# Attention's gates behind all pairs, and two of the convolution's four channel tiles on GpSimd

## What is computed

```python
for l in range(2):
    p = rms_norm(x, norm_w[l]) @ w_in[l]
    qa, ka, va, za, ub, zb, qkv_c, b_c, a_c, zc = split(p)
    oa = sliding_window_sink_attention(rope(norm(qa)), rope(norm(ka)), va, sinks[l]) * silu(za)   # 12 heads of 64
    a, gt = split(ub)                                # 512 channels each
    h = a * sigmoid(gt)
    h = causal_depthwise_conv(h, b_conv_w[l]) + b    # 31 taps over time, per channel
    ob = (silu(layer_norm(h)) @ pw_w[l] + pw_b[l]) * silu(zb)
    oc = rms_norm(gated_deltanet(qkv_c, b_c, a_c)) * silu(zc)   # has its own convolution of 4 taps
    x = x + concat(oa, ob, oc) @ w_out[l]
```

## Time and profile before

| | us |
|---|---|
| time, median of 3 runs (3611.47 to 3616.95) | 3613.13 |
| the profiled execution's own time | 3615.81 |
| its span, first to last instruction | 3614.0 |
| PE busy | 3472.0 |
| DVE busy | 2281.3 |
| ACT busy | 1851.8 |
| POOL busy | 155.6 |

### The profile page before, as it was taken

How to read it: one execution, slowest core, us unless ns; L and a number is a source line. 1 busy time by engine, 2 the same in 40 slices (tenths; PEclk the granted TensorE clock), 3 DMA queues, 4 the chain that set the end, 5 groups by cost and what they waited for, 6 DMA issues and landing times.

```text
span 3614.0 us, 41537 instructions
## 1 busy us (share of the span) xinstructions
PE 3472.0 (96%) x16074; PEld 2790.4 (77%) x16074; DVE 2281.3 (63%) x3126; ACT 1851.8 (51%) x2526; POOL 155.6 (4%) x243
## 2 busy tenths in 40 slices
PE   7988999988999999999999999999999999999998
PEld 5767778767778777788888888887777888888886
DVE  4956565966565656566666666656655566666665
ACT  4564555564555355655454454453566555445444
POOL 3014000013000000000000000000000000000000
PEclk9999999999999999999999999999999999999999
DMA  7434436434446345455655655653444565565564
GB/s 206 138 105 126 128 130 192 141 104 121 130 138 196 105 127 141 138 187 180 192 180 186 193 180 186 192 174 100 145 134 152 191 192 181 186 192 181 186 192 151
DMA packets 399092, 578.51 MB, mean 160 GB/s; under 512 B 25473, under 2 KB 222585, under 8 KB 398256
## 3 DMA queue, kind: packets, MB, share of 16 engines
q1 hardware_dynamic: 392544, 557.93, 50.4%
q0 software_dynamic: 5904, 16.75, 1.6%
q10 hardware_dynamic: 448, 1.18, 0.1%
HBM read 570.78 MB, written 4.98 MB: 159 GB/s over the span
## 4 chain that ended last, share of the span: by engine, by line
PE 82%; DVE 11%; ACT 4%; issue 2%; DMA 1%; DVEq 0%; ACTq 0%; SPq 0%
PE PS L706 79%; PE PS L703 3%; DVE WL L1844 3%; DVE ZA L2035 2%; ACT WH L1310 1%; DVE AR L1984 1%; DVE AR L2304 0%; ACT L1573 0%; DMA RAW<-in_w_in 0%; DVE SM L2243 0%; DMA X<-in_x 0%; DVE AR L2241 0%; ACT AR L1573 0%; ACT AR L1336 0%; ACT AR L1655 0%
## 5 line engine op out<-in xcount | busy, mean ns | idle before, releaser
L1844 DVE TENSOR_TENSOR WL<-RAW,WH 128x1024 fp32r<-128x1024 f32 x1056 | 1291.8, 1228 | 976.2 <-ACT WH L1310 973.6
L1310 ACT ACTIVATE WH<-RAW 128x1024 fp32r<-128x1024 f32 x1056 | 1105.1, 1056 | 965.6 <-PE PS L706 585.7
L706 PE MATMUL PS<-WH,Ah 128*128 128x512 f32 x3520 | 1431.9, 407 | 46.4 <-DVE WL L1844 32.9
L706 PE MATMUL PS<-WL,Ah 128*128 128x512 f32 x3520 | 1387.5, 394 | 0.0
L706 PE MATMUL PS<-WH,Al 128*128 128x512 f32 x3520 | 1387.4, 394 | 0.0
L706 PEld LDWEIGHTS PS<-WH,Ah 128*128 128x128 f32 x3520 | 671.9, 191 | 217.5 <-issue 40.8
L706 PEld LDWEIGHTS PS<-WL,Ah 128*128 128x128 f32 x3520 | 670.4, 190 | 145.4
L706 PEld LDWEIGHTS PS<-WH,Al 128*128 128x128 f32 x3520 | 672.3, 191 | 138.8 <-issue 6.8
L706 PE MATMUL PS<-WH,Zh 128*128 128x512 f32 x704 | 281.2, 399 | 0.0
L706 PE MATMUL PS<-WL,Zh 128*128 128x512 f32 x704 | 279.0, 396 | 0.0
L706 PE MATMUL PS<-WH,Zl 128*128 128x512 f32 x704 | 278.8, 396 | 0.0
(11 more groups left out here) (319 smaller groups left out, 2157.2 us busy)
## 6 DMA issues: line engine op xcount, KB each, us to landing
RAW<-in_w_in SPq DMA_DIRECT2D x368, 512.0 KB, 3.7
RAW<-in_w_up SPq DMA_DIRECT2D x704, 256.0 KB, 3.1
RAW<-in_w_down SPq DMA_DIRECT2D x176, 512.0 KB, 4.1
RAW<-in_w_out SPq DMA_DIRECT2D x64, 512.0 KB, 3.6
RAW<-in_w_o SPq DMA_DIRECT2D x64, 512.0 KB, 3.7
RAW<-in_w_in SPq DMA_DIRECT2D x64, 256.0 KB, 3.1
AR<-in_c POOLq DMA_DIRECT2D x2, 1600.0 KB, 7.6
AR<-bias_scratch POOLq DMA_DIRECT2D x16, 192.0 KB, 4.6
```

The lines of the kernel that those rows point to most:

```text
L706: return T.matmul(o, lhs, rhs, start=start, stop=stop, skip_group_check=True)
L1310: act(WH[:, j % NW, 0:n], raw_view(j), ACT.Copy).then_inc(*w_hi())
L1844: tt(WL[:, j % NW, 0:w], raw_view(j), WH[:, j % NW, 0:w].bitcast(F32), SUB).then_inc(*w_lo())
```

## The change

`C1CH` has zb ahead of za0. Attention's pipeline waits for va alone; DVE puts each pair's result times 0.5 into a new tile OA, and when the last pair is done and both gates are there, two products over all pairs put it into GT (gate0 over the two channel tiles of va's gate, gate1 over the four of za0); `merged` waits for gate1. In the convolution DVE keeps channel tiles 0 and 1. GpSimd does tiles 2 and 3 ahead of `base`: for each tap one product of HB with the tap into BTAP and one sum into ACC, each over both tiles, each waiting for the one before. PE's mean waits for both engines. ACT's part of DeltaNet behind the norms comes one pump later (12 + 9 instead of 12 + 8).

```diff
--- before.py
+++ after.py
@@ -209,7 +209,7 @@
 C1CH = [("uba", [(2048, 512)]), ("ubg", [(2560, 512)]), ("ba", [(5888, 12)]), ("qkv0", [(3584, 512)]), ("qkv1", [(4096, 512)]),
         ("qkv2", [(4608, 512)]), ("qa0", [(0, 512)]), ("qa1", [(512, 512)]), ("qkv3", [(5120, 512)]),
         ("qkv4", [(5632, 256), (5900, 256)]), ("zc", [(6156, 512)]), ("va", [(1024, 256), (1792, 256)]),
-        ("za0", [(1280, 512)]), ("zb", [(3072, 512)])]
+        ("zb", [(3072, 512)]), ("za0", [(1280, 512)])]
 C2CH = [("gqk", [(3072, 512)]), ("gv", [(3584, 512)]), ("ga", [(4608, 32)]), ("gr", [(4096, 512)]),
         ("dq0", [(0, 512)]), ("dk0", [(1024, 512)]), ("dv0", [(2048, 512)]), ("dq1", [(512, 512)]),
         ("dk1", [(1536, 512)]), ("dv1", [(2560, 512)]), ("rqk", [(4640, 512)]), ("rv", [(5152, 512)]),
@@ -421,7 +421,9 @@
         b_act = steps("b_act", per_layer(["id0", "id1", "id2", "id3", "sq", "vln", "vrs", "af0", "af1", "af2", "af3", "th",
                                           "pb0", "pb1", "pb2", "pb3"]))
         b_pe = steps("b_pe", per_layer(["mean", "var", "pw0", "pw1"]))
-        b_dve = steps("b_dve", per_layer([f"t{j}_{c}" for j in range(30) for c in R4] + ["mu", "cen", "nrm", "si", "out"]))
+        b_dve = steps("b_dve", per_layer([f"t{j}_{c}" for j in range(30) for c in R2] + ["mu", "cen", "nrm", "si", "out"]))
+
+        b_pool = steps("b_pool", per_layer([f"{n}{j}" for j in range(30) for n in "mt"]))
 
         items = [(t, h0) for t in (1, 0) for h0 in range(0, 12, 2)]
         aa_, ap, ad = ["sq", "ln", "rs"], [f"qt{c}" for c in range(5)], ["ss", "qn"]
@@ -441,6 +443,7 @@
             if 0 <= i - 3 < 12:
                 ap += [f"pv{i - 3}"]
                 ad += [f"gt{i - 3}"]
+        ad += ["gate0", "gate1"]
         a_act, a_pe, a_dve = steps("a_act", per_layer(aa_)), steps("a_pe", per_layer(ap)), steps("a_dve", per_layer(ad))
 
         fa, fp, fd = [], [], []
@@ -580,6 +583,8 @@
         KS, PW = za(1024, 2, 256), ar(14336, 4, 512)
         RT = [za(1024 + 128 * i, 128).rearrange("p (h d) -> p h d", d=8) for i in R4]
         SBUFS = [ar(12288 + 512 * i, 512) for i in R4]
+        OA = ar(0, 6, 256)
+        BTAP = ar(16384, 2, 256)
         OB = [ar(9216, 512), ar(0, 512)]
         OSQ = [ar(9728, 512), ar(512, 512)]
         TMP, TMF, ACC, HB, TB = za(0, 2, 512), za(0, 1024), za(1024, 4, 256), za(2048, 4, 256), za(2048, 4, 256)
@@ -857,7 +862,8 @@
                 yield from e.until("set up", "ubg")
                 for _ in range(31):
                     yield
-                T.wait_ge(*b_dve.at(m("t29_3")))
+                T.wait_ge(*b_dve.at(m("t29_1")))
+                T.wait_ge(*b_pool.at(m("t29")))
                 for c in R4:
                     ins = mm(bank(7, 256), ONES[:, :], ACC[:, c, :], c == 0, c == 3)
                 ins.then_inc(*b_pe(m("mean")))
@@ -1057,7 +1063,7 @@
                 T.wait_ge(*c_act.at(m("hl2")))
                 for i in range(15):
                     if i == 3:
-                        yield from e.until("va", "va.z", "za0")
+                        yield from e.until("va")
                     if i < 12:
                         t, h0 = items[i]
                         W = 128 + 128 * t
@@ -1097,6 +1103,8 @@
                                          SBUFS[(i - 3) % 4][:, o:o + 128], k == 0, k == t)
                         ins.then_inc(*a_pe(m(f"pv{i - 3}")))
                     yield
+                yield from e.until("va.z", "za0")
+                yield
                 e.flags.add("a")
 
             def gla(l):
@@ -1481,7 +1489,7 @@
                     if first:
                         A.wait_ge(*w_used.at(chunks[last_h[r]].end))
                         first = False
-                    A.wait_ge(*{"c": lambda: c_dve.at(f"{l}.hg12"), "b": lambda: b_dve.at(f"{l}.out"), "a": lambda: a_dve.at(f"{l}.gt11"),
+                    A.wait_ge(*{"c": lambda: c_dve.at(f"{l}.hg12"), "b": lambda: b_dve.at(f"{l}.out"), "a": lambda: a_dve.at(f"{l}.gate1"),
                                 "gla": lambda: g_dve.at(f"{l}.gg11"), "diff0": lambda: d_dve.at(f"{l}.og11"),
                                 "diff1": lambda: d_dve.at(f"{l}.og31"), "ret": lambda: r_dve.at(f"{l}.og11")}[name]())
                     for k in tiles:
@@ -1574,7 +1582,7 @@
                     A.wait_ge(*c_act.at(m(f"nln{r}")))
                     act(NS[r % 3], NS[r % 3], ACT.Exp, scale=-0.5).then_inc(*c_act(m(f"nrs{r}")))
                     yield
-                for _ in range(12 + 8):
+                for _ in range(12 + 9):
                     yield
                 for g in R3:
                     A.wait_ge(*c_pe.at(m(f"ta{g}")))
@@ -2027,7 +2037,7 @@
                 yield
                 for j in range(30):
                     d = 30 - j
-                    for c in R4:
+                    for c in R2:
                         if j == 0:
                             V.wait_ge(*b_act.at(m(f"id{c}")))
                         else:
@@ -2228,9 +2238,7 @@
                 yield from e.until("c")
                 for i in range(15):
                     if i == 3:
-                        yield from e.until("va", "va.z", "za0")
-                    if i == 3:
-                        V.wait_ge(*e_dve.at(m("za0.g")))
+                        yield from e.until("va")
                     if i < 12:
                         t, h0 = items[i]
                         W, b = 128 + 128 * t, i % 4
@@ -2256,10 +2264,16 @@
                         tt(s3, s3, ARS[b].unsqueeze(2).broadcast_to([128, 2, W]), MUL).then_inc(*a_dve(m(f"nm{i - 1}")))
                     if 0 <= i - 3 < 12:
                         t, h0 = items[i - 3]
-                        gt = GT[:, h0 // 2, 128 * t:128 * t + 128]
                         V.wait_ge(*a_pe.at(m(f"pv{i - 3}")))
-                        stt(gt, bank(4 + (i - 3) % 4, 128), 0.5, gt, MUL, MUL).then_inc(*a_dve(m(f"gt{i - 3}")))
-                    yield
+                        ts(OA[:, h0 // 2, 128 * t:128 * t + 128], bank(4 + (i - 3) % 4, 128), 0.5, None, MUL).then_inc(*a_dve(m(f"gt{i - 3}")))
+                    yield
+                yield from e.until("va.z", "za0")
+                V.wait_ge(*a_dve.at(m("gt11")))
+                for i, (j, name) in enumerate(((4, "va"), (0, "za0"))):
+                    V.wait_ge(*e_dve.at(m(name + ".g")))
+                    gt = GT[:, j:j + 4 - 2 * (j // 4), :]
+                    tt(gt, gt, OA[:, j:j + 4 - 2 * (j // 4), :], MUL).then_inc(*a_dve(m(f"gate{i}")))
+                yield
                 e.flags.add("a")
 
             def gla(l):
@@ -2565,6 +2579,15 @@
                     for h in range(8):
                         G.wait_ge(*u_dve.at(f"row{h}"))
                         G.dma_start(scr[h], BIASROW[h]).then_inc(scr_in, 16)
+                G.wait_ge(*b_act.at(f"{l}.id3"))
+                for j in range(30):
+                    n = 226 + j
+                    taps = P(("bcw", l), 4 * j + 2, 2).unsqueeze(2).broadcast_to([128, 2, n])
+                    if j > 0:
+                        G.wait_ge(*b_pool.at(f"{l}.t{j - 1}"))
+                    G.tensor_tensor(BTAP[:, :, 0:n], HB[:, 2:4, 0:n], taps, MUL).then_inc(*b_pool(f"{l}.m{j}"))
+                    G.wait_ge(*b_pool.at(f"{l}.m{j}"))
+                    G.tensor_tensor(ACC[:, 2:4, 256 - n:256], BTAP[:, :, 0:n], ACC[:, 2:4, 256 - n:256], ADD).then_inc(*b_pool(f"{l}.t{j}"))
                 base(l)
             for l in LL:
                 G.wait_ge(*p_lo.at(8 * (2 + 2 * l)))
```

## The result

The changed kernel took 3646.4 us, median of 4 runs (3645.59 to 3647.82), beside 3614.45 of the kernel before on the same chip (3611.47 to 3616.95). The ratio is 1.0098, with a 95% interval of 1.0086 to 1.0110: slower by some 32 us by the medians, or 35 by the ratio, where 47 were forecast. The profiled execution took 3646.66 with a span of 3644.8, 30.8 longer than before's.

A forecast was written before the change was run, and what follows sets the result against it. TensorE, busy 96% of the span, was taken to bound the kernel. Per layer, 27.5 (convolution) - 3 (attention) - 1 (ACT's place) = 23.5 us, 47 in all on the median 3613.1: 3660, range 3600 to 3700.

The forecast's parts named there:

- The mechanism: Convolution: DVE operations with two SBUF inputs take turns with GpSimd's; those with one PSUM input go untouched; +27.5 us a layer.
- The rival without turns: Convolution: scalar_tensor_tensor, or this shape, shares with GpSimd without loss; -18.3 us a layer, 3577; chance 0.18.
- GpSimd's operation, 1.13 us: Convolution on GpSimd: each product or sum takes 1.13 us at the mean of 482 elements, bounds 1.0 and 1.6.
- GpSimd becomes the wait: Mean after the convolution: at 2.2 us an operation it waits for GpSimd; +70 us a layer, 3750; chance 0.06.
- Price of a turn, 0.93: Convolution: a DVE operation loses all but 0.2 us of a GpSimd operation, 0.93 us for one of 1.13.
- Number of turns up to the first evacuation, 32: Pumps 0 to 8: 24 turns plus 4 at short operations plus 4 in the evacuation pump, costing 29.8 us.
- From there to GpSimd's end, +9.0: Six pumps after the first evacuation, 4.7 us each: 12.2 us later, less 3.2 of DVE's lead; PE 32.0 late.
- Second evacuation, -1.7: Convolution, GpSimd silent: the evacuation meets a lead of one pump only and costs 1.7 us less.
- Relief, 14.3: Convolution: halving DVE's steps gives PE back at most 14.3 us a layer, at the first three stalls and the mean.
- ACT one place later, -1: DeltaNet behind the norms: ACT issues its next weight tile before waiting for the transposes; -1 us a layer (0 to -2).
- Attention, -3: Attention's new order: 6.7 us saved at the change to the projection, some given back; net -3 a layer (0 to -7).
- The clock: Long convolution pumps: PE idle 2 of 4.7 us might lower its clock to 0.50; up to +7 us a layer, 3675.

The follow-up runs named there:

- experiment 5: Kernel before with all its DVE convolution steps, plus GpSimd's 60 operations a layer on a copy nobody uses, which PE's mean waits for: 3684.97 us, ratio 1.0199.
- experiment 8: Kernel before with only attention's new order (zb ahead of za0, gates behind all pairs), ACT at 12 + 8: 3609.43 us, ratio 0.9991.
- experiment 1: Kernel before with only the convolution of two channel tiles moved to GpSimd; attention and ACT's place as before: 3657.38 us, ratio 1.0135.
- experiment 3: Kernel before with only ACT's part of DeltaNet one pump later (12 + 9): 3602.17 us, ratio 0.9979.
- experiment 4: Changed kernel without GpSimd's convolution loop, leaving out all but the last tap of channel tiles 2 and 3: 3581.41 us, ratio 0.9927.
- experiment 6: Changed kernel with 120 GpSimd fills a layer in place of its products and sums, so it writes but reads nothing: 3578.98 us, ratio 0.9909.
- experiment 2: Changed kernel with all four channel tiles on DVE, keeping attention's new order and ACT's 12 + 9: 3601.21 us, ratio 0.9977.
- experiment 7: Changed kernel with one channel tile on GpSimd and three on DVE, 60 operations a layer of half the elements: 3611.53 us, ratio 0.9999.

## Why the prediction was right in kind and too high

PE's lateness in layer 0, tile by tile against the earlier trace rows, shows where the terms held. It sets one execution beside one, and the execution before is off in two places. From 94 to 97.5 us, ahead of GpSimd's first operation, it has a granted clock of 1.00, the changed kernel 0.57 and experiments 5 and 8 0.56 and 0.55; so its tile at 105.94 starts 1.0 to 1.5 us earlier than in the changed kernel and in experiments 1, 3, 5 and 8. From 265.75 to 388.90 it takes 4.0 to 4.2 us more than experiments 1, 5 and 8, whose kernels are those of the one before in this stretch. So some 1.3 us of the rows up to the mean is not the change's, and the last row is some 3 too low.

| place (start before, start after) | forecast | measured |
|---|---|---|
| tile after first evacuation (138.17, 156.04) | +23.0 | +17.9 |
| GpSimd's last operations (159.84, 184.82) | +32.0 | +25.0 |
| after the second evacuation (174.70, 199.89) | +30.3 | +25.2 |
| norm sums, third evacuation (191.42, 214.59) | +28.3 | +23.2 |
| mean (220.78, 243.16) | +27.5 | +22.4 |
| change to the projection (515.21, 529.12) | +23.5 | +13.9 |

- **The mechanism: right.** scalar_tensor_tensor takes turns like tensor_tensor, and L1994 with its input from PSUM takes none. Experiments 4 to 6 separate the turns from everything else. The rival without turns would have been experiment 4's ratio, 0.9927, or 3587 beside 3613 (forecast 3577). One thing is missing from the mechanism: the TENSOR_SCALAR with a single SBUF input was held as well.
- **GpSimd's operation, 1.13 us: right, slightly high.** Where nothing held it, it took 0.94 to 1.14, and 1.03 to 1.08 at the mean size. That 128 partitions are used instead of 48 shows in neither. It ended at 180.5, far ahead of the mean, and no PE wait names it, so *GpSimd becomes the wait* is out.
- **Price of a turn, 0.93: a little high.** Between 153.96 and 180.70 lie six pumps of 4.46 us. With 1.9 for the DVE work itself and three turns each that is (4.46 - 1.9) / 3 = 0.85. My 0.93 came from "all but 0.2" of an operation of 0.65, carried over to one of 1.13. The deduction held; the operation was shorter, mostly 1.05 to 1.14 in these pumps. Over all turns the 0.08 makes some 4 us a layer.
- **Number of turns up to the first evacuation, 32: too high, an error of the same size.** The subtraction at 153.96 starts 17.06 us later than that at 136.90. Of this 0.94 was there at 99.69 already (98.75 before) and comes from the slow tile at 94; the relief of 6.75 was used up as well. So the turns cost 17.06 - 0.94 + 6.75 = 22.9 us; the forecast had 29.8. At 0.85 a turn that is 27 turns, not 32: 2.6 us of the miss is the price, 4.3 the number. I had also left out the turn of the subtraction of 153.96 itself, which gives 0.8 back. The miss lies in pumps 0 to 7: from the subtraction at 99.69 to that at 141.87 they took 42.2 us and 28.5 before, so with 6.0 of relief 19.7 went to turns, where 28 turns at 0.93 make 26.0. GpSimd was as far as counted (34 of 60 operations had begun by 141.87, where I had 32), but more of its operations ran free: a step pair right behind the norm's L2116 and L2118, which read PSUM, took 1.53 or 1.82 us, not 2.5. I had charged a full three turns to every pump.
- **From there to GpSimd's end, +9.0: measured +7.1**, the price of a turn once more (six pumps of 4.46 us instead of 4.7).
- **Second evacuation, -1.7: measured +0.2.** PE waited 5.1 us at 192.78 and then lost 1.65 in a tile partly at low clock (4.37 instead of 2.72): 6.7, where the stall before cost 3.66 and 2.8. DVE, held until 180.5, came into it with about 1 us of lead, and I had not counted the slow tile. The third, -2.0, and the mean, -0.8, came as forecast (4.33 us of waiting instead of 5.12).
- **Relief, 14.3: measured 10.6.** It was my bound for the rivals. The first stall left 0.72 us and the second 0.92 (the evacuation alone is longer than DVE's lead), and the waits for ACT, from the third on, gave nothing back in sum, where I had 2. By the times of experiments 2 and 4 it is 9 to 10.
- **ACT one place later, -1: measured -3.8** (by the interval, -2.0 to -5.4), outside my 0 to -2. I took it that PE is idle for nothing at the transposes, and did not ask what else the earlier copy would bring forward: PE's wait of 2.06 us at 352.83. This is the step that failed outright.
- **Attention, -3: measured -1.6.** The trade was as told: the 3.0 at the change went, smaller waits inside the pairs came. In the changed kernel the longest wait of PE from 425 to 530 us is 1.8, so the bound of "no gap over 2 us" held.
- **The clock: not seen in the long pumps.** In the pumps of 4.46 us, of which a tile fills 2.72, tiles ran at the upper level: from 162 to 180 us the granted clock is 1.00, with PE busy 13.95 of 18. Only behind the gaps of 9.02 and 5.1 us did the first tile take 5.28 and 4.37 instead of 2.72, at a granted clock of 0.50 (156.04 to 161.30 and 192.78 to 195.90).

The 15 us between 47 and 32 come out as follows, per layer, with the 1.3 us taken off. The turns are 8.3 less (32.0 - 23.7): 4.0 by their price, 4.3 by their number. The second evacuation didn't save 1.9. Behind the mean PE regained 8.5 us in layer 0, of which some 4.1 is the slower stretch of the execution before; the 4.4 left stand beside the 4 that I had for attention and ACT's place (5.4 by the ratios of experiments 3 and 8). That is 8.3 - 1.9 + 0.4 = 6.8 a layer, and 16.7 of lateness instead of 23.5. Layer 1, whose last tiles are 16.8 later than layer 0's, agrees. So the 8.3 of the turns was in part hidden by the 1.9 of the second evacuation, and ACT's place (2.8 more gain than I had) and attention (1.4 less) missed in opposite directions. Both are luck.

## What to carry to other kernels

Before moving elementwise work from VectorE to GpSimd, count the VectorE operations with two SBUF inputs that will run beside it, and charge each nearly the length of one GpSimd operation; GpSimd's busy time alone says nothing of it. Beside these, a GpSimd operation that only writes went free here, as did one that reads while VectorE reads PSUM; shorter GpSimd operations cost less a turn. Ask of a reordering what else comes forward with it: one place in ACT's order gained 7 us here, where 120 steps taken off the busier engine lost 48.

## What the runs showed of the hardware

- Against DVE operations with two SBUF inputs, GpSimd's reads alone take turns. Its fills, 126.5 us of them, left these at 1228 and 461 ns (experiment 6). The Trainium skill ("SBUF — State Buffer", section "Who interferes with whom") says that a two-input VectorE instruction contends with a GpSimd instruction that reads SBUF, not with one that only writes it; the runs agree on both halves.
- The same page of the Trainium skill (section "SBUF: two separate sides") says that the one of the two that comes second is fully blocked for the whole instruction of the other. Measured, a turn costs 0.85 us beside operations of 1.0 to 1.14, and 0.43 to 0.53 beside 0.6: all but 0.1 to 0.3 us of GpSimd's operation. The rows fit that.
- A TENSOR_SCALAR from SBUF to SBUF, with one input, was held too: 1.13 us beside the sums and products (0.97 in experiment 5, 0.56 in experiment 7), 0.50 and 0.55 beside fills, 0.17 before. Some of these passed at 0.17, and RECIPROCAL, with one SBUF input, was never over 0.23. What sets the two apart, no run here shows.
- Both sides lose: GpSimd's 120 operations took 158.7 us (75.3 + 83.4), 1.32 each, against some 1.05 where nothing held them.
- Short operations pass in part. Behind DVE operations that read PSUM, two steps took 1.53 us instead of 2.5.

Not tried: holding GpSimd's operations back to the stretches in which DVE reads PSUM (L1994, L2116, L2118), and a product on GpSimd with one SBUF input.
